# The last weight unit in front of seven norms of a two-block transformer kernel, computed by token halves for both of its chunks

## The reference

```
def modulated_norm(x, g, shift, scale):
    return rmsnorm_2(x, g) * (1 + scale) + shift
...
h = modulated_norm(x, norm_g[l, 0], sh1, sc1)
x = x + 0.5 * g1 * swiglu(h, ffn_wg[l, 0], ffn_wu[l, 0], ffn_wd[l, 0])
h = modulated_norm(x, norm_g[l, 1], sh2, sc2)
```

## Time and profile before

| What | Before |
|---|---|
| Median of 3 runs | 2709.58 us (2709.11 to 2711.04) |
| The profiled execution's own time | 2709.57 us |
| Its span in the trace | 2707.7 us |
| PE busy | 2690.1 us, 99% of the span |
| DVE busy | 1432.9 us, 53% |
| ACT busy | 939.7 us, 35% |
| Granted TensorE clock | 1.00, 9 or more tenths in all 40 slices (its upper level, 2.4 GHz) |
| Chain that ended last | PE 98%, DVE 1%, ACT 1% |

### The profile page before, as it was taken

One profiled execution on the slowest core, in us unless ns is written; L12 is line 12 of the kernel. 1 busy time (PEld: TensorE's weight loads), 2 busy tenths in 40 slices (PEclk: granted clock), 3 DMA queues, 4 the chain that ended last, 5 costly groups with the idle time before them and its releaser, 6 DMA issues.

```text
span 2707.7 us, 32625 instructions
## 1 busy us (share of the span) xinstructions
PE 2690.1 (99%) x13009; PEld 2258.1 (83%) x13009; DVE 1432.9 (53%) x1607; ACT 939.7 (35%) x1180; POOL 71.2 (3%) x119
## 2 busy tenths in 40 slices
PE   8999999999999999999999999999999999999999
PEld 7888988888888888888878888888888888888887
DVE  7677554686667675657565333363333454533333
ACT  5555532433223422224554222243222332432222
POOL 1000000000000000001200000000000000000000
PEclk9999999999999999999999999999999999999999
DMA  4111222565555465654122322233322322233222
GB/s 142 63 62 62 79 94 93 180 224 205 198 198 179 148 213 198 215 186 129 58 68 83 104 93 93 88 99 97 105 93 93 94 94 94 94 104 97 93 93 78
DMA packets 257887, 323.73 MB, mean 120 GB/s; under 512 B 5766, under 2 KB 248708, under 8 KB 249604
## 3 DMA queue, kind: packets, MB, share of 16 engines
q1 hardware_dynamic: 245904, 245.12, 28.5%
q0 software_dynamic: 9216, 75.50, 7.5%
q10 hardware_dynamic: 2676, 1.84, 0.2%
HBM read 320.34 MB, written 2.10 MB: 119 GB/s over the span
## 4 chain that ended last, share of the span: by engine, by line
PE 98%; DVE 1%; ACT 1%; DMA 0%; issue 0%; SPq 0%; DVEq 0%
PE po L674 25%; PE po L676 25%; PE po L675 25%; PE po L844 2%; PE pm L874 2%; PE po L846 1%; PE po L845 1%; PE po L743 1%; PE po L745 1%; PE po L758 1%; PE po L791 1%; PE po L786 1%; PE po L777 1%; PE po L836 1%; PE po L837 1%; PE po L838 1%
## 5 line engine op out<-in xcount | busy, mean ns | idle before, releaser
L1957 DVE TENSOR_TENSOR w_lo<-w_raw,w_hi 128x1024 fp32r<-128x1024 f32 x472 | 561.8, 1220 | 446.8 <-ACT w_hi L1337 446.0
L1337 ACT ACTIVATE w_hi<-w_raw 128x1024 fp32r<-128x1024 f32 x470 | 476.9, 1051 | 883.4 <-PE po L676 862.6
L674 PE MATMUL po<-a_hi,w_hi 128*128 128x512 f32 x1840 | 716.5, 389 | 0.0
L676 PE MATMUL po<-a_hi,w_lo 128*128 128x512 f32 x1840 | 716.1, 389 | 0.0
L675 PE MATMUL po<-a_lo,w_hi 128*128 128x512 f32 x1840 | 716.1, 389 | 0.0
L676 PEld LDWEIGHTS po<-a_hi,w_lo 128*128 128x128 f32 x1840 | 345.4, 188 | 71.8
L675 PEld LDWEIGHTS po<-a_lo,w_hi 128*128 128x128 f32 x1840 | 345.5, 188 | 71.7
L674 PEld LDWEIGHTS po<-a_hi,w_hi 128*128 128x128 f32 x1840 | 345.5, 188 | 71.2
L674 PE MATMUL po<-b_hi,w_hi 128*128 128x512 f32 x1008 | 392.8, 390 | 0.0
L676 PE MATMUL po<-b_hi,w_lo 128*128 128x512 f32 x1008 | 392.4, 389 | 0.0
L675 PE MATMUL po<-b_lo,w_hi 128*128 128x512 f32 x1008 | 392.3, 389 | 0.0
(11 more groups left out here) (395 smaller groups left out, 2916.8 us busy)
## 6 DMA issues: line engine op xcount, KB each, us to landing
ada_in<-in_w_ada_dram POOLq DMA_DIRECT2D x64, 1152.0 KB, 5.6
w_raw<-in_ffn_wg_dram SPq DMA_DIRECT2D x44, 1024.0 KB, 5.3
w_raw<-in_ffn_wu_dram SPq DMA_DIRECT2D x44, 1024.0 KB, 5.3
w_raw<-in_w_ff_dram SPq DMA_DIRECT2D x32, 1024.0 KB, 5.6
w_raw<-in_ffn_wd_dram SPq DMA_DIRECT2D x32, 1024.0 KB, 5.3
w_raw<-in_w_in_dram SPq DMA_DIRECT2D x27, 1024.0 KB, 5.1
w_raw<-in_ffn_wd_dram SPq DMA_DIRECT2D x16, 768.0 KB, 4.8
w_raw<-in_w_in_c_dram SPq DMA_DIRECT2D x12, 1024.0 KB, 5.1
```

Of the source, the lines that this page charges most:

```text
L674: pe.matmul(o, wh, hi[:, k, :], start=(k == ks[0]), stop=False)
L676: mm = pe.matmul(o, wl, hi[:, k, :], start=False, stop=(k == ks[-1]))
L1337: act.activation(w_hi[:, s, part], w_raw[:, s, part], ACT.Copy).then_inc(hi_done, 1)
L1957: dve.tensor_tensor(w_lo[:, s, part], w_raw[:, s, part], w_hi[:, s, part].bitcast(F32), ALU.subtract).then_inc(lo_done, 1)
```

## The change

`product_tail` does the last unit in four parts: chunk 0 with H[0], chunk 1 with H[0], chunk 0 with H[1], chunk 1 with H[1]. The two parts for H[1] go to the banks `pm[:, 3]` and `pm[:, 2]`. All 256-column matmuls replace the 512-column ones of chunk 0. The two sum matmuls for H[0] now stand after 9 matmuls of the third part, which is chunk 0 with H[1]. DVE adds chunk 6 to `xT` in two halves, and ACT squares it in two halves ("sq6a", "sq6b"). The add of the squares for H[1], "add6b", moves behind "t1a", and "sq6b" stands in front of "hi0a". On ACT two more `a_hi` steps come before the logarithm for H[1]. In norm "00" the plain sum's add of chunk 6 moves to the low parts. Norms "00" and "01" get a wait for the modulation's sum, which uses `pm[:, 3]` too.

```diff
@@ product_tail, PE
-                for b, cols_ in ((0, slice(0, S)), (1, H[0]), (1, H[1])):
-                    for k in range(kc):
...
+                for half, cols_ in zip("ab", H):
+                    for b in range(2):
+                        first = half == "a" and b == 0
+                        o = po[:, slot, b, cols_] if half == "a" else pm[:, 3 - b, cols_]
+                        if half == "b" and b == 0 and name in ("00", "01"):
+                            pe.wait_ge(s_mod, mod_dve.after("mod", FFG - 1 if name == "00" else 2 * FFG - 2))
+                        for k in range(kc):
...
+                            if half == "b" and b == 0 and k == 2:
+                                pe.wait_ge(norm_dve[name].sem, norm_dve[name].after("add6a"))
+                                pe.matmul(pm[:, 0, H[0]], ones[:, :], ssq[:, H[0]], start=True, stop=False)
+                                pe.wait_ge(s_n_act, norm_act[name].after("sq7a"))
+                                pe.matmul(pm[:, 0, H[0]], last_gain(name), sq[:, 1, H[0]], start=False, stop=True)\
+                                    .then_inc(s_n_pe, norm_pe[name].one("suma"))
@@ norm_halves, ACT
+                for k in (DK - 2, DK - 1):
+                    act.wait_ge(s_tail_dve, tail_dve.after(f"{name}{'xy'[k % 2]}"))
+                    squares_added(k - 2)
+                    square(k, H[0], f"sq{k}a")
                 log("a")
                 root("a")
-                hi(0, "a")
-                hi(1, "a")
+                wait_x(act, name, DK - 2)
+                square(DK - 2, H[1], "sq6b")
+                for k in range(3):
+                    hi(k, "a")
                 wait_x(act, name, DK - 1)
                 square(DK - 1, H[1], "sq7b")
-                hi(2, "a")
                 hi(3, "a")
+                hi(4, "a")
                 log("b")
-                hi(4, "a")
                 hi(5, "a")
                 root("b")
@@ norm_halves, DVE
                 t(0, "a")
                 t(1, "a")
+                add_sixth(name, "b")
+                t(2, "a")
                 rest()
-                for k in range(2, DK):
+                for k in range(3, DK):
                     t(k, "a")
...
                     if name == "00" and k == 3:
+                        add_plain(DK - 2)
                         add_plain(DK - 1)
@@ residual, DVE
-                    dve.wait_ge(chunk_done, 2 * (u0 + v) + 1)
-                    gated(0).then_inc(out_taken[s], 1)
                     if v == 3 and then in TAIL:
-                        dve.wait_ge(s_tail_pe, tail_pe.after(then))
-                        gated(1, H[0]).then_inc(s_tail_dve, tail_dve.one(then))
-                        add_sixth(then)
+                        dve.wait_ge(s_tail_pe, tail_pe.after(f"{then}x"))
+                        gated(0, H[0]).then_inc(s_tail_dve, tail_dve.one(f"{then}x"))
+                        add_sixth(then, "a")
+                        dve.wait_ge(s_tail_pe, tail_pe.after(f"{then}y"))
+                        gated(1, H[0]).then_inc(s_tail_dve, tail_dve.one(f"{then}y"))
+                        dve.wait_ge(chunk_done, 2 * (u0 + 3) + 1)
+                        gated(0, H[1]).then_inc(out_taken[s], 1)
```

More of the change, by code:

```diff
@@ L321, in hybrid_two_block_kernel @@
                 continue
-            names = [f"sq{k}" for k in range(DK - 1)] + ["sq7a", "lna", "rstda", "hi0a", "hi1a", "sq7b"]
-            names += ["hi2a", "hi3a", "lnb", "hi4a", "hi5a", "rstdb", "hi6a", "hi7a"]
+            names = [f"sq{k}" for k in range(DK - 2)] + ["sq6a", "sq7a", "lna", "rstda", "sq6b", "hi0a", "hi1a", "hi2a"]
+            names += ["sq7b", "hi3a", "hi4a", "lnb", "hi5a", "rstdb", "hi6a", "hi7a"]
             names += [f"hi{k}b" for k in range(DK)]
@@ L327, in hybrid_two_block_kernel @@
             ba = norm_act[name].end
-            names = [f"add{k}" for k in range(DK - 1)] + ["add6b"] + [f"t{k}{half}" for half in "ab" for k in range(DK)]
+            names = [f"add{k}" for k in range(DK - 2)] + ["add6a", "t0a", "t1a", "add6b"]
+            names += [f"t{k}a" for k in range(2, DK)] + [f"t{k}b" for k in range(DK)]
             names += [f"lo{k}" for k in range(DK)]
@@ new lines, in product_tail @@
+                for half, cols_ in zip("ab", H):
[5 more added lines that the diff above has]
+                        for k in range(kc):
+                            if first and wait_k is not None:
+                                wait_k(k)
+                            if first and k == DK // 2:
+                                pe.wait_ge(lo_done, 2 * un + 2)
+                            wh = w_hi[:, slot, k * PAN + b * P:k * PAN + (b + 1) * P]
+                            wl = w_lo[:, slot, k * PAN + b * P:k * PAN + (b + 1) * P]
+                            pe.matmul(o, wh, hi[:, k, cols_], start=(k == 0), stop=False)
+                            pe.matmul(o, wh, lo[:, k, cols_], start=False, stop=False)
+                            mm = pe.matmul(o, wl, hi[:, k, cols_], start=False, stop=(k == kc - 1))
+                            if half == "b" and b == 0 and k == 2:
[4 more added lines that the diff above has]
+                                    .then_inc(s_n_pe, norm_pe[name].one("suma"))
+                        if half == "a":
+                            mm.then_inc(s_tail_pe, tail_pe.one(f"{name}{'xy'[b]}"))
+                        else:
+                            mm.then_inc(chunk_done, 1)
@@ L1373, in squares_added @@
                         act.wait_ge(s_fin_dve, fin_dve.after(f"p{k}"))
-                for k in range(DK - 1):
+                for k in range(DK - 2):
                     if k in (0, 2, 4):
@@ L1987, in add_plain, with add_sixth @@
                 ins.then_inc(s_fin_dve, fin_dve.one(f"p{k}"))
-            def add_sixth(name):
+            def add_sixth(name, half):
                 na, nd = norm_act[name], norm_dve[name]
+                c = H["ab".index(half)]
                 dve.wait_ge(nd.sem, nd.after(f"add{DK - 3}"))
[L1992 to L1999, removed]
-                if name == "00":
-                    add_plain(DK - 2)
+                dve.wait_ge(s_n_act, na.after(f"sq6{half}"))
+                if name == "00":
+                    ins = dve.scalar_tensor_tensor(ssq[:, c], sq[:, 0, c], square_gain[:, DK - 2:DK - 1], ssq[:, c],
+                                                   ALU.mult, ALU.add)
+                else:
+                    ins = dve.tensor_tensor(ssq[:, c], ssq[:, c], sq[:, 0, c], ALU.add)
+                ins.then_inc(nd.sem, nd.one(f"add6{half}"))
             def norm_halves(name, u0, rest):
@@ L2061, in residual @@
                         break
+                    dve.wait_ge(chunk_done, 2 * (u0 + v) + 1)
+                    gated(0).then_inc(out_taken[s], 1)
                     dve.wait_ge(chunk_done, 2 * (u0 + v) + 2)
```

14 lines of the change are left out of this document (6 added, 8 removed).

## The result

| What | Before | After |
|---|---|---|
| Median | 2709.52 us (2709.04 to 2711.04, 22 runs) | 2714.53 us (2713.28 to 2715.32, 22 runs) |
| Ratio to before, 95% interval | | 1.0017 [1.0011, 1.0023] |
| The profiled execution: time, span | 2709.57, 2707.7 us | 2714.36, 2712.5 us |
| Seven stretches together | 143.03 us | 148.12 us |

The change costs 5.0 us, 0.17%, where 4.1 us were forecast. It counts as within 0.2%, near the edge. The 22 runs of after fall into two groups by the granted clock: ten at 1.000 with a median of 2713.6 us (2713.28 to 2713.82), and twelve at 0.999 with 2715.0 us (2714.36 to 2715.32). The profiled execution is of the second group.

The account below looks back on a forecast made before the run. PE was taken to bound the kernel. Terms: -5.0 us (new minimum) + 8.5 (new waits) + 0.6 (restarts) = +4.1 us on 2709.57, forecast 2713.7 us; range 2708.0 to 2717.5 us.

Parts of the forecast that it names:

- What bounds the kernel: PE, busy 99% of the span; only the seven stretches around the norms change, everything outside is unchanged.
- The stretches: PE's seven spans, tail's first matmul to next step's first low-part matmul, one per norm: 19.7 to 23.6 us after the change.
- The split, 1.9 us: Chunk 0 on PE: 150 matmuls of 512 columns become twice as many of 256, 0.0125 us more each.
- The new minimum, 138.0: Seven stretches if PE waited nowhere, against 143.0 now: a win of 5.0 us, net of the split.
- The new waits, 8.5 us: At the two H[0] sums, PE waits for DVE's late chain: 2.61 in "ffn", 1.19 in "00", 1.52 or 0.08 elsewhere.
- Restarts, 0.6: PE starting again behind a wait at the sums costs 0.08 us, in seven norms.
- What no longer waits: PE's waits at L743 and k = 4 go; nothing taken for hi5a and hi6a, up to 0.1 us each norm kept.
- rival B: Waits in the first products stay, at hi5a behind H[1]'s logarithm: 3.0 us more, 2716.7 us; chance 0.25.
- Rival A: DVE is not late for the tail, which works as drawn: minus 5.0 us, 2704.6 us; chance 0.09.
- The bounds: Forecast alone: 2712.0 (no restart cost, chain 0.2 us shorter) to 2715.5 us (restart twice, 0.1 us more each norm).
- the clock is in no term: Rows of the kernel before show a granted clock of 1.00, so no term included it.

Follow-up runs that it names:

- experiment 4: Kernel before, with only chunk 0 of the last unit computed as two token halves, one right behind the other: 2711.98 us, ratio 1.0008.
- experiment 2: experiment 1, plus squares of chunks 4 and 5 added ahead of unit u0 + 4's weight parts on ACT and DVE: 2705.16 us, ratio 0.9984.
- experiment 1: Changed kernel, with DVE's 128x2304 accumulation in norm "ffn" moved from ahead of the squares to behind the norm: 2711.66 us, ratio to before 1.0008.
- experiment 8: Changed kernel, with DVE adding chunk 7 (H[0]) to `xT` before it adds the square of chunk 6: 2712.69 us, ratio to before 1.0011.
- experiment 5: Kernel before, with hi4a moved ahead of the logarithm for H[1] on ACT: 2707.34 us, ratio 0.9991.
- experiment 7: experiment 1, plus one 128x1024 DVE instruction in front of the squares in norm "10": 2713.97 us, ratio to before 1.0016.
- experiment 3: Kernel before with experiment 2's moves, `w_hi` behind the wait for chunk 6, `w_lo` behind both halves of the sixth add: 2716.59 us, ratio 1.0026.

## Why the prediction was right, and where it was off

- *What bounds the kernel.* Right: all of the difference lies in the seven stretches (+5.09 of stretch, +4.8 of span).
- *The stretches.* Forecast 23.6, 22.2, 19.7, 21.1, 19.7, 19.7, 21.1; measured 24.72, 22.16, 19.67, 21.11, 19.68, 19.67, 21.11. Six of seven are right to 0.1 us.
- *The split, 1.9 us.* Right to 0.2: 1.76 in experiment 4.
- *The new minimum, 138.0.* Right to 0.3: 137.77 when nothing waits (experiment 2). Its 0.53 for the first sum is a distance of the kernel before; in experiment 2 it is 0.43.
- *The new waits, 8.5 us.* Right in cause, and nearly in size: the stretches of after are 10.35 us longer than those of experiment 2, where nothing waits; less the 1.0 of the clock that is 9.4, where waits and restarts were put at 9.1. With the minimum 0.3 lower than forecast (137.77), two small errors cancel, and that the sum fits to 0.1 us at clock 1.000 is in part luck. L730 was put at 7.43 in "01" and came at 7.38; in "ffn" at 9.96 and came at 10.03. Experiments 1, 2 and 8 move the three pieces of the chain (what is ahead on DVE, and the order in it), and the waits follow each.
- *Restarts, 0.6.* In "01" L730 and the two matmuls behind it take 0.66 where 0.55 are due: 0.11 and 0.08 agree well enough, a term too small to test by a run.
- *What no longer waits.* Right: L743's wait is gone, and so are those at k = 4 and 6; neither hi5a nor hi6a came late. Experiment 5 gives them their price alone, 2.3 us in the stretches, with 0.1 left in each norm at k = 6; together that is the 3.0 of rival B, which fell.
- *Rival A* is refuted for this change, and reached by experiment 2 (2705.16, where A said 2704.6).
- *The bounds.* The forecast's own upper bound of 2715.5 is 0.5 more than its terms give: 0.6 for a second restart and 7 x 0.1 lead from 2713.7 to 2715.0. No reading hangs on it.
- *The step that failed* is the sentence "the clock is in no term". It was read from rows of a kernel whose PE waited 0.7 us at most in these stretches, and the forecast itself put a wait of 2.6 us there. The granted clock fell to 0.50 behind it, for about 1.0 us of loss in the profiled execution and 1.4 us between the two groups of runs. Those at clock 1.000 have 2713.6 us against the forecast 2713.7; the sum holds where its condition holds. Why the clock falls in one execution and not in the next stays open.

## What to carry to other kernels

Taking a sum or a handover earlier on the bound engine pays only if the engine that produces its input is free by then; so read, for the producer, what stands ahead of it in its queue, and take the later of "operand ready" and "queue free" as the start of the chain. Here PE delivered 2.2 to 2.9 us into the stretch and DVE came at 5.0 to 7.6, and that difference, with the clock that fell behind the longest wait, was the whole result: 2705.2 us with DVE on time, 2714.5 without. A moved instruction must stand in front of the waits it doesn't need, and a control for it must do the same, or it measures its own mistake (experiment 3).

## What was not expected of the hardware

- The clock fell behind waits of PE as short as 2.0 and 2.1 us (experiment 7 and the changed kernel), and only in a part of the executions of one and the same kernel: 12 of 22, 7 of 11, 6 of 11. In the profiled executions, no wait of 0.6 to 1.2 us in these stretches had a fall behind it, nor had the waits of 1.3 and 1.5 us at the start of after. The kernel before showed 0.999 too, in 2 of 33 executions (2710.0 and 2710.1 us) and 1 of 31 (2711.9 us); none of these three was profiled, so no trace shows where. What makes one execution fall and the next not was not found, and waits between these lengths, or of 2 us without transfers beside them, were not tried.
- In a timeline of PE a float32 sum that starts late can show no idle time at all: L730 came 0.31 us late with no bracket (experiment 8 took the wait away). Only the difference of starts shows it.
